# A decoder layer's expert stage: pairs of experts in rounds of 64 columns, changed to two expert streams in four equal groups of 32 columns, with a sorted load list and rolled loops

## The chip, the cores and the metric

One core of one Trainium2 chip runs the kernel. The metric is device time in microseconds for one launch. The core has TensorE (PE in the profile; PEld is its weight load), VectorE (DVE), ScalarE (ACT), GpSimd (POOL) and SyncE (SP), which here only issues DMAs.

## What is computed

One layer of a hybrid decoder for 512 prompt tokens and 8 sample tokens, d_model 1024, all in float32: adaLN modulation, an input projection to an RG-LRU half and a sliding-window attention half, an RMS norm of each half with a gain (`g_lru`, `g_attn`), an output projection, a residual layer norm, and then the expert layer, which the change is mostly about:

```python
def hier_moe(h, w_group, b_group, w_router, b_router, w_gate, w_up, w_down):
    pg = softmax(h @ w_group + b_group)                  # 4 groups
    g_val, g_idx = top_k(pg, 1)                          # one group for each token
    pe = softmax(logits of the 8 experts of that group)
    e_val, e_idx = top_k(pe, 2)                          # two experts in it
    weight = g_val * e_val / sum(e_val)
    expert = g_idx * 8 + e_idx                           # 32 experts
    z = silu(h @ w_gate[e]) * (h @ w_up[e]) * combine    # 1024 -> 256
    return sum over e of z @ w_down[e]                   # 256 -> 1024
```

520 tokens with two experts each are 1040 rows, over 32 experts of 3.15 MB of weights (three matrices of 1 MB), some 100 MB. The biases of the inputs make the groups unequal.

## The kernel before

The kernel is written engine by engine, with semaphores by hand; each engine's instructions run in the order of its function. The stages follow each other: modulation and input projection, LRU and attention, output projection with residual and norm in five tiles, router, expert stage, and the weighted sum of each token's two rows with the last norm.

**Attention half.** For each of four blocks of 128 queries VectorE masks scores (L1050), ScalarE makes exponentials (L770), TensorE transposes the weights, ScalarE evacuates these (L784), TensorE multiplies with the values (L1527) and VectorE's `store_O` copies the result out of PSUM into `yT` (L1076). After the last block ScalarE squares the four attention rows of `yT` (L795), TensorE sums the squares (L1577), VectorE makes a mean of the sums (L1114), multiplies the four attention rows with the gain `g_attn` (L1116) and takes a reciprocal (L1118), TensorE transposes it (L1583), and the output projection goes on (L1596).

**Routing.** VectorE finds the two experts of each token, TensorE counts the tokens of each expert and their ranks, and VectorE turns these into slots in a table in DRAM. The table has a column for each step and a row for each of the 128 columns of a step. Ten indirect stores by GpSimd write it (L590), one load brings it back (`idx_all`), and the gathers of token rows begin.

**Expert stage.** The 32 experts are 16 fixed pairs. A step handles up to 64 tokens of each expert of a pair: columns 0 to 63 belong to the one, 64 to 127 to the other. A pair with an expert of more than 64 tokens takes more steps. Three buffers hold a pair's weights each (`wex`, `SETS = 3`); SyncE loads pairs in order, gate and up when the gate-up of the pair that last used the buffer is done (`gu_ps`), down when its down projection is done (`y_ps`) (`load_pair`, L439 to L446). Two pairs and a part of the third are loaded ahead of the stage. On TensorE, step n does:

```python
for k in range(KD):                    # gate-up, L1680: 8 k-slices x 2 column groups
    for q in range(2):
        matmul(B[2 + j % 2][64*q : 64*q + 64, :], XT[:, j % 2, k, 64*q : 64*q + 64], gate and up of q, slice k)
transpose_X((j + 1) % RING, i, 0)      # first half of the next step's tokens, L1661
transposes of z                        # L1687, wait for silu (ACT, L842) and multiply (DVE, L1297)
transpose_X((j + 1) % RING, i, 1)
for k in range(2):                     # down, L1699: 2 k-slices x 2 banks x 2 column groups
    for c in range(2):
        for q in range(2): ...
```

The profile records each float32 matmul as two. VectorE and ScalarE copy half of y each (L1302, L849). GpSimd gathers the tokens of a step with an indirect DMA from `h_dram` into `X` (L608, L610) and scatters a step's y into `y_dram` with another (L619, L621). `X` and `yo` are rings of four (`RING`), the gather is three steps ahead (`AHEAD`): in each step GpSimd first gathers for step s + 3, then waits for the y copies of step s and scatters.

**Control.** Which buffer a step's pair lies in is known only on the chip: each step reads three registers (L1669 to L1671) and picks one of three arms by `If` (L1673). Four steps (a turn) are written out in the body of a loop; the first turn is peeled, three follow in a loop (L1708), and the rest up to `TURNS` = 8 stand in a loop whose body is guarded by `If(nturns > i)` (L1711, L1712). All engines go through the whole range and skip what isn't wanted (VectorE L1309, ScalarE L856, GpSimd L640). When GpSimd is through it waits for the last stores and sets `mark` (L648), SyncE reloads y (`yy`), and TensorE sums it (L1722).

## Time and profile before

| | us |
|---|---|
| median of three runs (662.65 to 664.29) | 663.6 |
| time of the profiled execution | 662.54 |
| its span, first to last instruction | 660.5 |
| PE busy | 539.1 (82%) |
| PEld busy | 274.0 (41%) |
| DVE busy | 229.9 (35%) |
| ACT busy | 159.1 (24%) |
| POOL busy | 124.3 (19%) |
| DMA, 168.97 MB | mean 256 GB/s |

The chain that ended last goes 63% by PE, 12% by DVE, 9% by DMA and 6% by the issue of DMAs on SyncE. Times in rows are microseconds from the first instruction; "mean ns" is that of one instruction. "128*64" is the shape of the part of TensorE's array that a matmul uses. An engine name with a q is its sequencer, which loads registers and branches ahead of the work that it has queued; such rows do not count as busy. In a row of a line's instructions three durations stand as least, median and most. "[4.13 <-DMA x]" is idle time of the engine ahead of the row and what ended it. For DMAs the last number is the time from issue to landing.

### The profile page before, as it was taken

What the parts mean: (1) busy time and instruction counts of PE and PEld (TensorE: products, weight loads), DVE (VectorE), ACT (ScalarE), POOL (GpSimd) and SP (SyncE); (2) the same over time, 40 slices, a digit from 0 to 9 for tenths busy, and PEclk for the clock granted to TensorE, in tenths of its full rate; (3) what the DMA queues carried; (4) which work ended last, traced back from release to release, by engine and by line L of the source; (5) the groups of instructions that cost most, each with busy time, mean ns of one, the idle gap of its engine ahead of it and who ended that gap; (6) DMA issues with size and microseconds to landing.
All of it is one profiled execution on the core that took longest, in us unless ns stands there. A gap on an engine that the chain in (4) does not pass through costs nothing.

```text
span 660.5 us, 7214 instructions
## 1 busy us (share of the span) xinstructions
PE 539.1 (82%) x2420; PEld 274.0 (41%) x2421; DVE 229.9 (35%) x524; ACT 159.1 (24%) x332; POOL 124.3 (19%) x186
## 2 busy tenths in 40 slices
PE   1879999999988799961079899989999978789391
PEld 0458777887434344430033334334333323233130
DVE  0331444323394588998011111111111101011178
ACT  1221444525465111220011111111211101011054
POOL 5020010000543440020621121112112111111000
PEclk9969999999799899986579999999999989789795
DMA  8993945401846812119379968249999999996432
GB/s 276 407 363 136 319 163 195 155 4 32 323 171 228 326 46 89 64 36 389 155 261 405 423 251 328 114 188 417 420 418 420 420 419 421 416 411 226 172 130 98
DMA packets 46004, 168.97 MB, mean 256 GB/s; under 512 B 13178, under 2 KB 22450, under 8 KB 30590
## 3 DMA queue, kind: packets, MB, share of 16 engines
q1 hardware_dynamic: 36682, 146.48, 56.6%
q0 software_dynamic: 8944, 21.87, 9.3%
q8 instruction: 27, 0.44, 0.3%
q10 hardware_dynamic: 340, 0.09, 0.1%
q14 instruction: 11, 0.09, 0.0%
HBM read 165.18 MB, written 18.32 MB: 278 GB/s over the span
## 4 chain that ended last, share of the span: by engine, by line
PE 63%; DVE 12%; DMA 9%; SPq 6%; issue 5%; ACT 3%; POOL 1%; POOLq 0%; DVEq 0%
PE B L1680 18%; PE B L1432 16%; PE B L1699 8%; PE B L1596 5%; DMA wex<-in_w_up 4%; PE B L1369 3%; SPq L372 3%; DMA x_tok<-in_x_sample 2%; PE B L1501 2%; SPq L374 1%; SPq L371 1%; PE B L1661 1%; PE B L1687 1%; PE B L1444 1%; PE B L1527 1%
## 5 line engine op out<-in xcount | busy, mean ns | idle before, releaser
L1680 PE MATMUL B<-wex,XT 128*64 128x512 f32 x640 | 149.7, 618 | 19.2 <-DMA wex<-in_w_up 11.2
L1432 PE MATMUL B<-hT,win 128*128 128x256 f32 (+1 forms) x448 | 104.1, 393 | 2.0 <-DVE hT L953 2.0
L1680 PEld LDWEIGHTS B<-wex,XT 128*64 128x64 f32 x640 | 52.9, 142 | 113.8 <-issue 112.0
L1432 PEld LDWEIGHTS B<-hT,win 128*128 128x128 f32 x448 | 86.2, 195 | 22.5 <-issue 9.3
L1699 PE MATMUL B<-wex,zT 128*64 128x512 f32 x320 | 73.1, 598 | 0.6
L1297 DVE TENSOR_TENSOR z<-silu_g,B 128x256 f32<-128x256 f32 x20 | 8.4, 422 | 162.0 <-ACT silu_g L842 162.0
L1661 PE MATMUL B<-ident,X 128*128 128x128 f32 x168 | 28.4, 294 | 26.8 <-DMA X<-h_dram,gidx 26.8
L1596 PE MATMUL B<-wout,yT 128*128 128x512 f32 x112 | 50.1, 605 | 0.0
L842 ACT ACTIVATE silu_g<-B 128x256 f32<-128x256 f32 x20 | 7.7, 386 | 153.5 <-PE B L1680 153.5
L1302 DVE COPY yo<-B 128x512 f32<-128x512 f32 x20 | 13.8, 692 | 83.1 <-PE B L1699 83.1
L619 POOL COPY sidx<-idx_all 128x1 int32 (+1 forms) x20 | 3.6, 182 | 198.8 <-DVE yo L1302 198.8
L1661 PEld LDWEIGHTS B<-ident,X 128*128 128x128 f32 x168 | 22.7, 196 | 43.1 <-issue 43.1
L1699 PEld LDWEIGHTS B<-wex,zT 128*64 128x64 f32 x320 | 21.2, 136 | 38.7 <-issue 34.3
L1596 PEld LDWEIGHTS B<-wout,yT 128*128 128x128 f32 x112 | 21.5, 195 | 26.6 <-issue 26.6
L1722 PE MATMUL B<-yy,wdiag 128*128 128x512 f32 (+1 forms) x40 | 21.5, 699 | 10.2 <-DMA yy<-y_dram 10.0
L610 POOL DMA_INDIRECT X<-h_dram,gidx x23 | 24.1, 1048 | 20.0 <-POOL gidx L608 18.8
L849 ACT ACTIVATE yo<-B 128x512 f32<-128x512 f32 x20 | 12.0, 598 | 62.2 <-PE B L1699 62.2
L565 POOL TENSOR_SCALAR P<-P,rden 128x256 f32<-128x256 f32 (+1 forms) x16 | 14.4, 914 | 59.4 <-DVE rden L1064 59.4
L1369 PE MATMUL B<-ada,cT 128*32 128x512 f32 x160 | 24.0, 704 | 1.7 <-issue 1.0
L621 POOL DMA_INDIRECT y_dram<-yo,sidx x20 | 20.3, 1016 | 17.3 <-POOL sidx L619 17.3
L1289 DVE COPY XT<-B 128x512 f32<-128x512 f32 x21 | 14.4, 684 | 20.3 <-PE B L1661 20.3
L534 POOL DMA_DIRECT2D ada<-in_w_ada x12 | 6.7, 563 | 77.5 <-PE B L1369 77.5
(327 smaller groups left out, 585.0 us busy)
## 6 DMA issues: line engine op xcount, KB each, us to landing
wex<-in_w_gate SPq DMA_DIRECT2D x32, 1024.0 KB, 16.8
wex<-in_w_up SPq DMA_DIRECT2D x32, 1024.0 KB, 19.3
wex<-in_w_down SPq DMA_DIRECT2D x32, 1024.0 KB, 20.4
ada<-in_w_ada POOLq DMA_DIRECT2D x12, 1024.0 KB, 7.4
ada<-in_w_ada SPq DMA_DIRECT2D x8, 1024.0 KB, 8.2
win<-in_w_in SPq DMA_DIRECT2D x7, 1024.0 KB, 14.0
wout<-in_w_out SPq DMA_DIRECT2D x1, 4096.0 KB, 13.1
yy<-y_dram SPq DMA_DIRECT2D x8, 512.0 KB, 6.7
```

The costliest lines, as they stand in the source:

```text
L372: sp.dma_start(to[:, q, KD * DE:GU], u_).then_inc(got, 16)
L565: pool.tensor_scalar(Pm[b % 3][:, h, keys], Pm[b % 3][:, h, keys], rden[:, b % 2, h:h + 1], None, ALU.mult).then_inc(P_ready, 1)
L610: pool.indirect_dma_start(X[:, j, :], None, h_dram[:, :], bass.IndirectOffsetOnAxis(ap=gidx[:, j:j + 1], axis=0), bounds_check=NT - 1, oob ...
L621: pool.indirect_dma_start(y_dram[:, :], bass.IndirectOffsetOnAxis(ap=sidx[:, j:j + 1], axis=0), yo[:, j, :], None, bounds_check=2 * NT - 1 ...
L1289: dve.tensor_copy(XT[:, s % 2, 0:4, :], B[0][:, :].rearrange("p (k m) -> p k m", m=P)).then_inc(XT_v, 1)
L1369: last = pe.matmul(B[7 if r == 2 else 4][32 * g:32 * g + 32, :], cT[:, k, :], w[:, g * 512:(g + 1) * 512], start=(k == 0), stop=(k == KD - 1))
L1432: last = pe.matmul(B[(q % 2) * 2 + h][:, 0:cn], win[:, n % 3, k, col:col + P], hT[:, k, c0:c0 + cn], start=(k == 0), stop=(k == KD - 1))
L1596: last = pe.matmul(B[2 * g + c][:, :], yT[:, FW * g + f, t * P:(t + 1) * P], wout[:, FW * g + f, c * 512:(c + 1) * 512], start=(f == 0), s ...
L1661: last = pe.transpose(B[half][:, (k % 4) * P:(k % 4 + 1) * P], X[:, j, k::KD], ident[:, :])
L1680: last = pe.matmul(B[2 + j % 2][64 * q:64 * q + 64, :], XT[:, j % 2, k, 64 * q:64 * q + 64], gu[:, :, k, :], start=(k == 0), stop=(k == KD ...
L1699: last = pe.matmul(B[5 + c][64 * q:64 * q + 64, :], zT[:, k, 64 * q:64 * q + 64], wex[pl][:, q, dn:dn + 512], start=(k == 0), stop=(k == 1))
L1722: last = pe.matmul(B[2 * (t % 2) + c][0:n, :], wdiag[0:n, t, e, 0:n], yy[0:n, t, e, c * 512:(c + 1) * 512], start=(e == 0), stop=(e == 1))
```

## The change

- The experts of group 0 (0 to 7) form stream A; the other 24 form 12 fixed pairs, stream B. A step works on one A expert in two lanes of 32 columns (rounds of `WA` = 64 tokens) and on one B pair in one lane each (rounds of `WB` = 32 tokens). Both streams advance by themselves; the number of steps is that of the longer. `MAXSTEP` becomes 44.
- Weights: three buffers for single A experts, the third in the place of the output projection's weights (region `w`), two for B pairs. Three A experts and two pairs are loaded ahead of or at the start of the stage. The 15 later loads are sorted on VectorE by the step that first needs them; SyncE reads the list entry by entry.
- `X`, `XT` and `yo` have one buffer each in place of four, two and four, in region `y`. GpSimd gathers for step s + 1 when step s's tokens are transposed, then scatters step s.
- All loops have one step as their body; TensorE has six arms (three A places times two B places) instead of three, and one loop from 0 to `MAXSTEP`.
- In the attention half `g_attn` is multiplied in as the results leave PSUM (`gA`), and ScalarE squares each block out of PSUM once VectorE has stored it; the four multiplications behind the sums go.

```diff
-CAP = 64
...
-RING = 4
-AHEAD = RING - 1
...
+NA, NB = EPG, (NE - EPG) // 2
+NU = NA + NB
+WA, WB = 64, 32
+
+MAXSTEP = max((2 * NT + (WA - 1) * NA) // WA, (2 * NT + (WB - 1) * NB) // WB)
+MINSTEP = max(NA, NB)
...
+ABUF, BBUF = 3, 2
...
-        X = row("X", [P, RING, D], "w", 0)
-        XT = row("XT", [P, 2, KD, P], "w", 16384)
+        X = row("X", [P, D], "y", 0)
+        XT = row("XT", [P, KD, P], "y", 8192)
...
-        yo = row("yo", [P, RING, D], "y", 0)
+        yo = row("yo", [P, D], "y", 4096)
...
+        wA = [row("wA0", [P, EXW], "r", 0), row("wA1", [P, EXW], "r", 4 * EXW), row("wA2", [P, EXW], "w", 0)]
+        wB = [row("wB0", [P, 2, EXW], "x", 0), row("wB1", [P, 2, EXW], "r", 8 * EXW)]
...
-            sp.wait_ge(lgT_ps, 2)
-            load_expert(2, 1, 0)
+            sp.wait_ge(L_ps, TT + 1)
+            sp.wait_ge(A_ps, TT)
+            load_a(2)
+            sp.wait_ge(x1_stored, 16 * (TT + 1))
+            load_b(0, 0)
+            load_b(0, 1)
             sp.wait_ge(lg_ps, 1)
...
-            load_expert(3, 1, 1)
...
-            load_expert(4, 2, 0, (True, False))
-            sp.wait_ge(X_in[AHEAD - 1], 16)
-            load_expert(4, 2, 0, (False, True))
-            load_expert(5, 2, 1)
+            load_b(1, 0)
+            sp.wait_ge(X_in, 16)
+            load_b(1, 1)
...
+            with sp.Fori(0, LATER) as n:
+                free = sp.value_load(loads_i[0:1, 1, bass.ds(n, 1)], min_val=1, max_val=MAXSTEP)
+                place = sp.value_load(loads_i[0:1, 2, bass.ds(n, 1)], min_val=0, max_val=ABUF + BBUF - 1)
+                e = sp.value_load(loads_i[0:1, 3, bass.ds(n, 1)], min_val=0, max_val=NE - 2)
...
+                for b in range(BBUF):
+                    with sp.If(place == ABUF + b):
+                        sp.wait_ge(gu_ps, free)
+                        for q in range(2):
+                            later_expert(e + q, wB[b][:, q, :], (True, False), wB_in[b])
+                        sp.wait_ge(y_ps, free)
+                        for q in range(2):
+                            later_expert(e + q, wB[b][:, q, :], (False, True), dB_in[b])
...
+            def one(s):
+                pool.wait_ge(XT_ps, counted(2 * s + 2))
+                gather(s + 1, 2 * s + 1)
+                scatter(s)
+
+            gather(0, 0)
+            one(0)
+            with pool.Fori(1, MINSTEP) as s:
+                one(s)
...
+            nsteps = pool.value_load(steps_i[0:1, 0:1], min_val=MINSTEP, max_val=MAXSTEP)
+            with pool.Fori(MINSTEP, MAXSTEP) as s:
+                with pool.If(nsteps > s):
+                    one(s)
+
+            ends = [pool.value_load(ends_i[0:1, j:j + 1], min_val=16 * MINSTEP, max_val=16 * (MAXSTEP + 1)) for j in range(2)]
+            pool.wait_ge(y_out, ends[0])
+            pool.wait_ge(X_in, ends[1])
...
+            def squares(b):
+
+                act.wait_ge(O_stored, 2 * (b + 1))
+                act.activation(qT[:, :, b * P:(b + 1) * P], B[6][:, :].rearrange("p (g q) -> p g q", q=P), ACT.Square).then_inc(sq_ready, 1)
+
             for b in range(TT + 1):
                 if b < TT:
                     exps(b)
+                if b >= 2:
+                    squares(b - 2)
                 if b >= 1:
                     evacuate_PT(b - 1)
...
-            for f in range(FW, 2 * FW):
-                act.activation(sq[:, f, :], yT[:, f, :], ACT.Square).then_inc(sq_ready, 1)
+            squares(TT - 1)
...
-                        i = dve.tensor_copy(yT[64 * half:64 * half + 64, FW + 2 * kv:FW + 2 * kv + 2, b * P:(b + 1) * P],
...
+                        i = dve.tensor_tensor(yT[64 * half:64 * half + 64, FW + 2 * kv:FW + 2 * kv + 2, b * P:(b + 1) * P],
...
-            for f in range(FW, 2 * FW):
-                dve.tensor_scalar(yT[:, f, :], yT[:, f, :], par[:, 32 + f:33 + f], None, ALU.mult).then_inc(yg_ready, 1)
...
+                    pe.wait_ge(sq_ready, FW + b)
...
+            def lanes(a, b):
+
+                return [wA[a], wA[a], wB[b][:, 0, :], wB[b][:, 1, :]]
+
+            def one(n):
+                arm = pe.value_load(arm_i[0:1, bass.ds(n, 1)], min_val=0, max_val=ABUF * BBUF - 1)
...
+                for a in range(ABUF):
+                    for b in range(BBUF):
+                        with pe.If(arm == BBUF * a + b):
...
+                            pe.wait_ge(wA_in[a], need_a)
+                            pe.wait_ge(wB_in[b], need_b)
                             for k in range(KD):
...
+                                for g, w in enumerate(lanes(a, b)):
+                                    gu = w[:, 0:GU].rearrange("p (c k f) -> p c k f", c=2, k=KD)
+                                    last = pe.matmul(B[2][32 * g:32 * g + 32, :], XT[:, k, 32 * g:32 * g + 32],
                                                      gu[:, :, k, :], start=(k == 0), stop=(k == KD - 1))
                             last.then_inc(gu_ps, 1)
...
+                            pe.wait_ge(X_in, 16 * n + 32)
+                            transpose_X(0)
                             pe.wait_ge(z_ready, n + 1)
...
+            nsteps = pe.value_load(steps_i[0:1, 0:1], min_val=MINSTEP, max_val=MAXSTEP)
+            with pe.Fori(0, MAXSTEP) as n:
+                with pe.If(nsteps > n):
+                    one(n)
```

## Rows read from the trace of the kernel before

**Rows 1.** Page, part 2: 40 equal slices of the span.
```profile
DMA  8993945401846812119379968249999999996432
GB/s 276 407 363 136 319 163 195 155 4 32 323 171 228 326 46 89 64 36 389 155 261 405 423 251 328 114 188 417 420 418 420 420 419 421 416 411 226 172 130 98
```

**Rows 2.** Timeline, first gate-up of the expert stage.
```profile
336.50 8.49 PE L1680 MATMUL B<-wex,XT 128*64 128x512 f32 x32 [0.73 <-ACT XT L836]
```

**Rows 3.** Timeline, behind the last step.
```profile
616.37 1.04 POOL L621 DMA_INDIRECT y_dram<-yo,sidx  x1 [0.86 <-POOL sidx L619]
...
619.17 0.10 POOL L648 MEMSET mark<- 128x1 f32 x1 [1.76 <-DMA y_dram<-yo,sidx]
...
624.37 2.04 PE L1722 MATMUL B<-yy,wdiag 128*128 128x512 f32 x2 [10.01 <-DMA yy<-y_dram]
```

**Rows 4.** Timeline of one step, all engines: start, duration, engine, line.
```profile
423.50 0.71 PE L1661 MATMUL B<-ident,X 128*128 128x128 f32 x4
...
424.51 0.51 PE L1687 MATMUL B<-ident,z 128*128 128x128 f32 x2 [0.29 <-DVE z L1297]
...
425.49 3.65 PE L1699 MATMUL B<-wex,zT 128*64 128x512 f32 x16
...
429.19 0.69 DVE L1302 COPY yo<-B 128x512 f32<-128x512 f32 x1 [4.13 <-PE B L1699]
...
431.15 1.02 POOL L621 DMA_INDIRECT y_dram<-yo,sidx  x1 [0.86 <-POOL sidx L619]
...
433.21 1.05 POOL L610 DMA_INDIRECT X<-h_dram,gidx  x1 [0.84 <-POOL gidx L608]
```

**Rows 5.** DMA issues, one gather each, windows 415:428, 402:415 and 441:454.
```profile
X<-h_dram,gidx POOLq DMA_INDIRECT x1, 3.3
...
X<-h_dram,gidx POOLq DMA_INDIRECT x1, 8.3
...
X<-h_dram,gidx POOLq DMA_INDIRECT x1, 9.7
```

**Rows 6.** Chain that ended last: modulation in four lanes, clock low, then full.
```profile
174.06 6.03 PE B L1369 x32
...
186.42 1.85 PE B L1369 x16
```

**Rows 7.** Timeline of PE, two gate-ups behind waits for weights.
```profile
536.61 8.78 PE L1680 MATMUL B<-wex,XT 128*64 128x512 f32 x32 [4.13 <-DMA wex<-in_w_up]
...
552.94 7.09 PE L1680 MATMUL B<-wex,XT 128*64 128x512 f32 x32 [1.98 <-DMA wex<-in_w_up]
```

**Rows 8.** Page, part 3, then sequencer rows of single lines: arms, loops.
```profile
q8 instruction: 27, 0.44, 0.3%
...
L1673 PEldq COMPARE_BRANCH  x60: 68/207/5084, 336.0 to 611.2; - x60
...
L1708 PEldq COMPARE_BRANCH  x3: 76/207/223, 440.8 to 547.5; - x3
...
L1711 PEldq ALU_OP  x4: 36/36/36, 611.4 to 613.8; - x4
...
L640 POOLq ALU_OP  x4: 32/32/32, 616.1 to 617.5; - x4
```

**Rows 9.** Timeline, attention's third block and what follows the last.
```profile
204.05 1.78 DVE L1076 COPY yT<-B 64x256 f32<-64x256 f32 x4 [1.33 <-PE B L1527]
...
204.63 1.09 ACT L784 ACTIVATE PT<-B 128x512 f32<-128x512 f32 x2 [2.70 <-PE B L1518]
...
215.76 5.93 DVE L1116 TENSOR_SCALAR yT<-yT,par 128x520 f32<-128x520 f32 x4
...
223.46 0.69 PE L1583 MATMUL B<-ident,rs 128*128 128x128 f32 x2 [4.47 <-DVE rs L1118]
```

**Rows 10.** DMA issues, stores of the table, windows 313.5:315 and 324:325.
```profile
table<-pair_id,slot POOLq DMA_INDIRECT x2, 6.2
...
table<-pair_id,slot POOLq DMA_INDIRECT x1, 1.9
```

More of the change, by code:

```diff
@@ L195, in build @@
         par = small("par", [P, 40])
+        gA = small("gA", [P, G])
         stT = small("stT", [P, FW, 32])
@@ L405, in _ @@
             sp.wait_ge(win_ps, 2 * len(ORDER))
-            for q in range(2):
-                load_expert(q, 0, q)
+            for i in range(2):
+                load_a(i)
             sp.wait_ge(ss_sum_ps, 1)
@@ L625, in turn @@
-            def turn(i, peeled):
-                for j in range(RING):
-                    s = RING * i + j
-                    if not (peeled and j == 0):
-                        pool.wait_ge(XT_ps, counted(2 * s))
-                    gather((j + AHEAD) % RING, s + AHEAD, AHEAD + 2 * s)
-                    scatter(j, s)
-            for s in range(AHEAD):
-                gather(s, s, s)
-            turn(0, True)
-            with pool.Fori(1, MINTURNS) as i:
-                turn(i, False)
@@ L638, in _ @@
-            pool.wait_ge(steps_ready, 1)
-            nturns = pool.value_load(turns[0:1, 0:1], min_val=MINTURNS, max_val=TURNS)
-            with pool.Fori(MINTURNS, TURNS) as i:
-                with pool.If(nturns > i):
-                    turn(i, False)
-            scattered, gathered = counted(16 * nturns, 16 * nturns + 16)
-            for j in range(RING):
-                pool.wait_ge(y_out[j], scattered)
-                pool.wait_ge(X_in[j], gathered if j < AHEAD else scattered)
-            pool.memset(mark[:, :], 0.0).then_inc(experts_done, 1)
+                pool.tensor_copy(sidx[:, :], idx_all[:, bass.ds(s, 1), 1]).then_inc(idx_ready, 1)
@@ L860, in row_stats @@
+            copy_XT(0)
+            one(0, True)
+            with act.Fori(1, MINSTEP) as n:
+                one(n, False)
+            nsteps = act.value_load(steps_i[0:1, 0:1], min_val=MINSTEP, max_val=MAXSTEP)
+            with act.Fori(MINSTEP, MAXSTEP) as n:
+                with act.If(nsteps > n):
+                    one(n, False)
             def row_stats(t, n):
@@ L1093, in _ @@
                 if b == 1:
+                    for kv in range(NKV):
+                        for half in range(2):
+                            step(dve.tensor_copy(gA[HD * kv:HD * kv + HD, half::2],
+                                                 par[HD * half:HD * half + HD, 32 + FW + 2 * kv:32 + FW + 2 * kv + 2]))
+                    settle()
                     dve.wait_ge(sO_ps, 1)
@@ L1243, in _ @@
[L1243 to L1247 removed]
+            step(dve.tensor_scalar(unum_i[:, 0, 0:NA], B[5][:, 0:NA], 1.0, float(WA - 1), ALU.max, ALU.add))
+            link(dve.tensor_reduce(umax[:, NA:NU], B[5][:, NA:NE].rearrange("p (a b) -> p a b", b=2), AX.X, ALU.max))
@@ L1279, in _ @@
[L1279 to L1284 removed]
+            step(dve.tensor_copy(uend_i[:, :], uend[:, :]))
@@ L1313, in _ @@
+            copy_XT(0)
+            one(0, True)
+            with dve.Fori(1, MINSTEP) as n:
+                one(n, False)
+            nsteps = dve.value_load(steps_i[0:1, 0:1], min_val=MINSTEP, max_val=MAXSTEP)
+            with dve.Fori(MINSTEP, MAXSTEP) as n:
+                with dve.If(nsteps > n):
+                    one(n, False)
             for t, n in TILES:
```

388 lines of the change are left out of this document (204 added, 184 removed).

## The prediction

> **What bounds the kernel now.** I read the forty slices of the page first, to find the stretch that matters: from about 330 us on the kernel is in its expert stage, and there the DMA engines are full from slice 28 to 36 at 411 to 421 GB/s but not in slices 24 to 27, where they carry 328, 114 and 188 GB/s [rows 1]. So neither engine binds throughout: while experts 4 to 7 take three steps a pair, TensorE binds and the weight stream sleeps; after that the stream binds. The stage runs from the first gate-up at 336.5 us [rows 2] to 614.4 us (the last output store is issued at 616.4, 2.0 us behind the last matmul) [rows 3], 277.9 us for 20 steps, and 46.1 us follow it. Then one step in order of time, for the chain that the change shortens to one buffer: transposes of the next tokens, of z, the down projection of 3.65 us, the y copy, the store of y issued 2.0 us after the last matmul, and the gather of tokens issued 4.1 us after it [rows 4]. Now this gather is three steps early, so nobody sees how long it takes. Last, how long it takes: 3.3 us from issue to landing where the weight queue is empty, 8.3 us with it just filled, 9.7 us with it full [rows 5].
>
> **Fewer steps.** The reference's router on its inputs gives experts 0 to 7 these tokens: 57 29 51 33 137 103 163 91; the pairs behind them have maxima 25 11 20 14 20 40 39 36 7 9 7 6. Before: sixteen pairs in rounds of 64, 20 steps (two with three rounds). After: stream A needs 1+1+1+1+3+2+3+2 = 14 rounds of 64, stream B 1+1+1+1+1+2+2+2+1+1+1+1 = 15 rounds of 32; they run beside each other, so 15 steps.
>
> **A step on TensorE.** Four lanes of 32 columns replace two of 64. The page has four such lanes elsewhere: two chunks of the modulation, 16 records, take 1.85 us [rows 6], 0.925 us for one k-slice of four lanes. Gate-up: 8 x 0.925 = 7.4 us (7.1 now [rows 7]); down: 4 x 0.925 = 3.7 us. Between gate-up and down lie 1.99 us [rows 4]. Sequencer work between steps (three register loads, up to five skipped arms, the loop's branch) hides under the down projection as now; I add 1.1 us exposed for the longer chain of arms. A step on TensorE alone: 1.1 + 7.4 + 2.0 + 3.7 = 14.2 us.
>
> **The gather, now late.** There is one X and one yo. GpSimd issues the gather of step n+2 only after the store of step n. Issue is 4.1 us after the last matmul of step n, 4.3 with its loop's branch. Landing is between 3.3 and 9.7 us, as weights are in flight or not; I take 9.0 under load. TensorE wants it 1.1 + 7.4 = 8.5 us after that last matmul, and it comes at 13.3: a hole of 4.8 us in the middle of the step. Behind it are the transposes (0.72 us without their wait on z, then 0.98) and down 3.7: 5.4 us. A hole of such length also lowers the granted clock: the gate-up behind 4.13 us idle took 8.78 us against 7.09 behind 1.98 us [rows 7], so 1.7 us. A loaded step: 4.3 + 9.0 + 5.4 + 1.7 = 20.4 us. Who else waits on that one X: only TensorE; the single yo asks for a store that lands about 10 us after the step before, which is early.
>
> **Which steps are loaded.** After the seven experts that are in place, 25 of 3.15 MB remain, at 420 GB/s 7.5 us each, 187 us, and some 20 us for X and y. The first steps free A and a pair together (22.5 us of transfers in a step of 20.4), so steps 1 to 5 are loaded. Later a step frees a pair or nothing. Behind a short step that freed one, the gather meets gate, up and down in full: steps 9 and 11. Behind a long step only the down part is left: steps 6, 7, 12 and 13, between 14.2 and 20.4, I take 16.0. Behind the second round of a pair nothing moves: steps 8, 10, 14, 14.2 us. Step 0 starts at the low clock as now, 8.49 us of gate-up [rows 2]: 14.6. Sum: 14.6 + 7 x 20.4 + 4 x 16.0 + 3 x 14.2 = 264.0 us, against 277.9: 13.9 us less, although five steps of about 13.9 went. The weights are no bound: 207 us of transfers in 264.
>
> **The end of the loops.** Nobody says stop: each engine walks the range to MAXSTEP, now 44, and skips. Before, three turns were skipped; now 29 steps. A skip costs GpSimd (617.5 - 616.1) / 3 = 0.47 us and TensorE (613.8 - 611.4) / 3 = 0.8 us [rows 8]. GpSimd's begin 1.7 us after the last matmul: 1.7 + 29 x 0.47 + 1.6 for two register loads = 16.9 us until the mark that releases the reload of y, which stood at 4.8 us (619.17) [rows 3]. TensorE's last 23.2 us but begin 3 us before that matmul, so they end at 20.2, ahead of the y that lands at 22.1 instead of 10.0 [rows 3]. Cost: 12.1 us, cover none. The Trainium skill (Advanced Engine Details and Errata, Control Flow Timing) gives about 108 ns to a compare-and-branch; two of them 29 times would be 6.3 us on each engine and the cost would be 3 to 5 us, an estimate from that page. The spacing in the rows counts the whole iteration, and the sum goes by it.
>
> **Ahead of the stage.** The gain of the attention half moves into the copies out of PSUM, so the four VectorE scalings of 5.93 us go; TensorE idled 4.47 us for what stood behind them, and all of that is won [rows 9]. Against it: ScalarE's square of a block now waits for VectorE's store (204.05 + 1.78) and stands ahead of the next evacuation, which began at 204.63 [rows 9]: 1.8 us in the third block, 0.2 in the second, and 0.4 for the extra copies of the samples. Net 2.0 us won (bounds 0 and 4.5). Routing: five more small VectorE operations ahead of the slots, 0.8 us; the some 35 more behind them (sorting loads) take 8 us and end some 10 us before X lands. More weights are asked for in this window: 12.6 MB from 295 us, until 325. GpSimd's last table store, at 324.0 now, then meets them; loaded ones took 6.2 us, it takes 1.9 now [rows 10]: I take 2.3 more, bounds 0 and 4.3. SyncE is moved past nothing that it waits for. Together 1.1 us lost.
>
> **Sum.** -13.9 + 1.1 + 12.1 = -0.7 us. The profiled execution has 660.5 us span and 662.54 us of time, so 661.8; the median of the runs is 1.1 higher, 663.6, and I forecast 663. 0.3% (2 us) is about what a measurement of this kernel can tell from no change.
>
> **Rivals.**
> (a) The late gather as above (0.54), 663; by itself 645 to 682: landing at 8.3 takes 7 us off, at 9.7 it adds 6, an exposed 3 us between steps adds 4, no clock loss takes 9 off. This case lies on both sides.
> (b) The gather is not late (0.15): with weights in flight only 80% of the time it lands in about 3.3 us, steps go at 14.2 and the last weights set the end. Some 223 us of stage (207 of transfers and the ends): 41 less, 622. Against it: 8.3 us already stood where the queue had been filled only 5 us before.
> (c) Slower: the clock (0.25). The hole is in the middle of a step, and behind it come sparse transposes, so the low level lasts through the down projection. At the low level four lanes need 1.5 us (6.03 / 4) for what takes 0.925 [rows 6], so down costs 6.0 and the transposes 0.9 more: 3.2 in place of 1.7 us, in nine steps with a hole: 13.5 us, 676. It decides from 2.0 us per hole on. For it: step 0, where transposes after a long idle did not lift the clock and the gate-up still lost 1.4 us (8.49 against 7.09) [rows 2, 7].
> (d) Slower: code loading (0.06). TensorE took up to 5.08 us in one branch over an arm, but 0.08 to 0.22 in the loop's own branch back [rows 8]; the queue of instructions moved 27 packets, 0.44 MB in all, once per piece of code [rows 8]. If each step lost 2.4 us twice, all 15 steps would take about 20.3 us: 304 us, 703. The Trainium skill (Runtime: NRT & Kernel Launch, Instruction fetch mechanics) says that a taken branch out of the fetched window stalls for a fetch, and would make this the likely case with a jump in every step; the trace's loop of twelve arms, larger than the new one of six, ran back without it.
> Chances: (a) gives 0.26 faster, 0.13 same, 0.15 slower; with (b), (c) and (d): faster 0.41, same 0.13, slower 0.46. Range 642 to 685: it holds (a) and (c), and leaves out (b) and (d).
>
> **What would show it.** 15 silu and 15 yo copies. TensorE's transposes of X wait on the DMA of X, 4 to 5 us in steps 1 to 5 and next to nothing in 8, 10 and 14; if these waits are absent, (b). Gate-up near 7.4 us, down near 3.7; down near 5 or 6 means (c). Stage near 264 us. Mark some 17 us after the last matmul, y's sum some 22 us after it; if it stays at 10, the skip price is wrong. Scalings of yT gone and 4.47 us of idle with them. Gaps over 2 us between down and gate-up with the weights landed would mean (d). Wrong altogether would be a step count other than 15, or weights as the last wait through the middle of the stage.

## The result and the profile after

The changed kernel takes 702.1 us (median of 4 runs, 696.4 to 703.3) beside 663.9 us of the kernel before: ratio 1.0565, 95% interval 1.0490 to 1.0639, so some 5.7% slower. The 663.9 is the median of four runs, of which one took 1134.0 us; the ratio leaves that one out, and the other three have 663.6. The forecast was 663 with a range of 642 to 685, and 0.46 for slower.

The profiled execution's span is 701.2 us, 40.7 more than before. Three stretches hold them. The stage begins at 337.85 us instead of 336.50 [rows 2]: 1.35 us more. It lasts until the last matmul at 643.2: 305.4 us instead of 277.9, 27.5 more. And 58.0 us follow instead of 46.1: 11.9 more. The first and the last are what the prediction said (1.1 and 12.1). The stage should have come to 264.0 and took 41.4 us more than that.

The page of the kernel after, slices of 17.5 us (the stage is slices 19 to 36, counted from 0), the instruction queue, and the two parts that name the stage's costs, the chain and the groups:

```profile
PE   1889999998979998600814865658696867774091
...
PEclk9979999999899999855765988999889898988585
...
GB/s 278 403 370 101 324 127 234 65 0 244 251 97 419 44 91 62 112 423 268 285 414 136 315 423 416 413 421 202 353 66 412 182 405 362 360 101 84 112 161 92
...
q8 instruction: 15, 0.25, 0.1%
...
PE 50%; DMA 19%; issue 12%; DVE 11%; ACT 3%; POOL 2%; POOLq 2%; SPq 0%; DVEq 0%
...
L1761 PE MATMUL B<-wA,XT 128*32 128x512 f32 x480 | 112.8, 624 | 49.5 <-issue 49.5
...
L1740 PE MATMUL B<-ident,X 128*128 128x128 f32 x128 | 29.4, 373 | 79.2 <-DMA X<-h_dram,gidx 79.2
...
L1780 PE MATMUL B<-wA,zT 128*32 128x512 f32 x240 | 64.0, 682 | 0.2
```

Before, the DMA engines stood at 411 to 421 GB/s in nine slices on end [rows 1]; now they do so in four. PE is at 9 in one slice of the stage alone, and its granted clock is below 9 tenths in eleven of the eighteen. So through most of the stage neither the matmuls nor the weights set the pace. L1740, the transposes of X, wait 79.2 us for the gather (30.1 of them once, ahead of the stage). And L1761, the gate-up, waits 49.5 us for "issue", time in which the engine waited for nothing that the profile shows. More than half of that is one piece. Timeline of all engines from the end of step 0, the SyncE queue left out (start, duration, engine, line; in brackets the idle time before it and what ended it):

```profile
353.07 0.69 DVE L1378 COPY yo<-B 128x512 f32<-128x512 f32 x1 [4.14 <-PE B L1780]
...
356.99 1.05 POOL L645 DMA_INDIRECT X<-h_dram,gidx  x1 [0.84 <-POOL gidx L643]
378.41 1.07 PE L1761 MATMUL B<-wA,XT 128*32 128x512 f32 x2 [25.41 <-issue]
```

Between step 0 and step 1 TensorE stands still for 25.41 us. Its sequencer rows on L1753, the `If` over the arms, in three windows (count; ns least/median/most; first and last start):

```profile
L1753 PEldq COMPARE_BRANCH  x2: 5690/5986/6281, 350.7 to 357.0; - x2
...
L1753 PEldq COMPARE_BRANCH  x2: 5638/5648/5658, 362.8 to 368.5; - x2
...
L1753 PEldq COMPARE_BRANCH  x78: 68/200/217, 394.5 to 640.7; - x78
```

Four branches, at 350.7, 357.0, 362.8 and 368.5 us, take 6.28, 5.69, 5.64 and 5.66 us: 23.3 us, of which the first 2.3 lie under the down projection. The 4.2 us from the last of them to the first matmul are the sequencer's ordinary work for a step: the branch back, three table loads of 0.30 us with their register operations (374.8 to 377.2), and the short branches to the arm. In the later steps most of this lies under the down projection: 21.9 us of it show in 13 steps, 1.7 each (1.1 predicted). Later, 78 branches of the same line take 217 ns at most. From 353 to 378 us the instruction queue moves 5 packets, 0.08 MB; I read them as the code of arms that step 0 did not run. The same stretch as a window (length; busy time of PE, PEld, DVE, ACT, POOL; then granted clock, DMA share and GB/s):

```profile
353.00:378.40 25.40, 0.00 (x0) 0.02 (x1) 0.69 (x1) 0.60 (x1) 2.44 (x4) 0.57 0.83 340
```

TensorE does nothing in it, its clock is granted at 0.57, near the lower of its two levels (1.2 of 2.4 GHz), and the weights go on at 340 GB/s in the mean (400 from 357 to 374 us, next to nothing after that).

The other steps, from the y copies of VectorE (L1378): steps 2 to 14 last 22.8, 21.3, 20.7, 20.6, 14.6, 22.0, 13.9, 20.9, 14.5, 22.5, 15.1, 21.8 and 18.7 us. Step 2, the chain of waits in order of time:

```profile
396.93 0.21 POOL gidx L643
397.25 0.49 issue
397.78 0.19 issue
397.96 10.89 DMA X<-h_dram,gidx
408.90 1.12 PE B L1740 x4
410.02 0.43 PE B L1768 x2
410.44 0.85 PE B L1740 x4
411.30 5.28 PE B L1780 x32
416.60 0.04 DVEq L1377
```

The gather is issued 4.2 us after step 1's last matmul, lands 10.89 us later, and all behind it follows at once. The ten later landings on this chain take 10.2, 9.9, 9.9, 10.3, 4.3, 9.9, 11.1, 5.6, 9.7 and 8.2 us. Last, what follows the stage, GpSimd's mark and TensorE's sum, where [rows 3] had them at 619.17 and 624.37:

```profile
645.30 1.01 POOL L655 DMA_INDIRECT y_dram<-yo,sidx  x1 [0.86 <-POOL sidx L653]
659.33 0.19 POOL L676 TENSOR_TENSOR mark<-mark 128x1 f32<-128x1 f32 x1 [13.01 <-issue]
664.69 3.75 PE L1800 MATMUL B<-yy,wdiag 128*128 128x512 f32 x4 [21.52 <-DMA yy<-y_dram]
```

### The profile page after: what moved, and what is told of

It is laid out like the page before. It is cut to its first block, busy times and chain, and to the rows that moved or that the text cites. A ratio compares the mean times of both kernels' runs of the same rounds, so it can differ in the third digit from the quotient of the medians.

```text
span 701.2 us, 8747 instructions
## 1 busy us (share of the span) xinstructions
PE 492.4 (70%) x2850; PEld 251.3 (36%) x2851; DVE 223.7 (32%) x544; ACT 149.0 (21%) x313; POOL 107.7 (15%) x167
## 4 chain that ended last, share of the span: by engine, by line
PE 50%; DMA 19%; issue 12%; DVE 11%; ACT 3%; POOL 2%; POOLq 2%; SPq 0%; DVEq 0%
DMA X<-h_dram,gidx 15%; PE B L1508 15%; PE B L1780 9%; PE B L1670 5%; PE B L1761 5%; PE B L1740 3%; PE B L1445 3%; DMA x_tok<-in_x_sample 2%; PE B L1577 2%; DVE yo L1378 1%; PE B L1639 1%; PE B L1520 1%; PE B L1800 1%; PE B L1768 1%; POOL table L625 1%
## 5 line engine op out<-in xcount | busy, mean ns | idle before, releaser
L1761 PE MATMUL B<-wA,XT 128*32 128x512 f32 x480 | 112.8, 624 | 49.5 <-issue 49.5
L1761 PE MATMUL B<-wB,XT 128*32 128x512 f32 x480 | 112.8, 625 | 0.0
L1508 PEld LDWEIGHTS B<-hT,win 128*128 128x128 f32 x448 | 86.3, 195 | 22.5 <-issue 9.3
L1740 PE MATMUL B<-ident,X 128*128 128x128 f32 x128 | 29.4, 373 | 79.2 <-DMA X<-h_dram,gidx 79.2
L1761 PEld LDWEIGHTS B<-wA,XT 128*32 128x32 f32 x480 | 33.8, 114 | 125.3 <-issue 125.3
L1780 PE MATMUL B<-wA,zT 128*32 128x512 f32 x240 | 64.0, 682 | 0.2
L1780 PE MATMUL B<-wB,zT 128*32 128x512 f32 x240 | 64.0, 682 | 0.0
L1740 PEld LDWEIGHTS B<-ident,X 128*128 128x128 f32 x128 | 22.1, 210 | 92.6 <-DMA X<-h_dram,gidx 60.8
L1800 PE MATMUL B<-yy,wdiag 128*128 128x512 f32 (+1 forms) x40 | 21.5, 699 | 21.7 <-DMA yy<-y_dram 21.5
L1378 DVE COPY yo<-B 128x512 f32<-128x512 f32 x15 | 10.4, 692 | 72.9 <-PE B L1780 72.9
L1367 DVE COPY XT<-B 128x512 f32<-128x512 f32 x16 | 11.0, 690 | 69.5 <-PE B L1740 69.4
L1780 PEld LDWEIGHTS B<-wA,zT 128*32 128x32 f32 x240 | 14.1, 124 | 39.6 <-issue 35.3
L1761 PEld LDWEIGHTS B<-wB,XT 128*32 128x32 f32 x480 | 27.7, 114 | 0.0
L599 POOL TENSOR_SCALAR P<-P,rden 128x256 f32<-128x256 f32 (+1 forms) x16 | 14.5, 918 | 59.9 <-DVE rden L1094 59.9
L879 ACT ACTIVATE yo<-B 128x512 f32<-128x512 f32 x15 | 9.0, 597 | 56.4 <-PE B L1780 56.4
## 6 DMA issues: line engine op xcount, KB each, us to landing
wA<-in_w_gate SPq DMA_DIRECT2D x8, 1024.0 KB, 12.7
```

The costliest lines, as they stand in the source:

```text
L599: pool.tensor_scalar(Pm[b % 3][:, h, keys], Pm[b % 3][:, h, keys], rden[:, b % 2, h:h + 1], None, ALU.mult).then_inc(P_ready, 1)
L879: act.activation(yo[:, 512:D], B[6][:, :], ACT.Copy).then_inc(y_a, 1)
L1367: dve.tensor_copy(XT[:, 0:4, :], B[0][:, :].rearrange("p (k m) -> p k m", m=P)).then_inc(XT_v, 1)
L1378: dve.tensor_copy(yo[:, 0:512], B[5][:, :]).then_inc(y_v, 1)
L1508: last = pe.matmul(B[(q % 2) * 2 + h][:, 0:cn], win[:, n % 3, k, col:col + P], hT[:, k, c0:c0 + cn], start=(k == 0), stop=(k == KD - 1))
L1740: last = pe.transpose(B[half][:, (k % 4) * P:(k % 4 + 1) * P], X[:, k::KD], ident[:, :])
```

## The experiments

Three theories, one for each loss. **Skips**: the tail's 12 us are 29 passes that are tested and skipped. **Code**: the hole of 25.4 us is the fetching of arms, once, and each fetch is slow since weights fill the DMA engines. **Order**: the long steps are the gather's, and not for being slow but for being issued behind the end of the step before. Times are medians; after each, the ratio to the kernel before, with its interval.

### e1_range15: nothing to skip

```diff
-            with pool.Fori(MINSTEP, MAXSTEP) as s:
+            with pool.Fori(MINSTEP, 15) as s:
```
and so for ScalarE, VectorE and TensorE.

> The change, with the loops over steps of all four engines ending at 15 instead of 44: these inputs make 15 steps, so nothing of the work is left out, only the 29 passes that each engine skips. Main theory (skipped passes cost 0.47 us each on GpSimd, 0.8 us on TensorE, and lie on the path behind the last step): GpSimd's mark comes 3 us behind the last matmul instead of 16.1, the last down projection stays near 643 us, the tail of 58.0 us shrinks by 12 to 46, and the time by 12 us, 702 to 690. Rival (the skips run beside the last scatter's landing and the last weights' wait, so something else is late next): under 4 us gained.

689.4 us (1.0405, 1.0381 to 1.0430), 12.7 less. The profiled execution is the shortest of the five, 684.85 us. GpSimd's last scatter and mark, and TensorE's sum:

```profile
638.93 1.06 POOL L656 DMA_INDIRECT y_dram<-yo,sidx  x1 [0.86 <-POOL sidx L654]
641.81 0.19 POOL L677 TENSOR_TENSOR mark<-mark 128x1 f32<-128x1 f32 x1 [1.82 <-DMA y_dram<-yo,sidx]
647.22 12.95 PE L1801 MATMUL B<-yy,wdiag 128*128 128x512 f32 x25 [10.44 <-DMA yy<-y_dram]
```

13.01 us of "issue" before the mark have become 1.82 us behind the scatter, and TensorE's wait for y 10.44 instead of 21.52. The mark is 5.0 us behind the last matmul (3 were expected; before it was 4.8), and 46 us follow that matmul instead of 58.0. The skips were the tail's whole loss; the late gathers (45.4 us of waits in 11 steps) and the hole (26.4 us here) stayed.

### e2_dry15: the code fetched ahead of the stage

```diff
+            pool.memset(arm_i[:, 0:1], ABUF * BBUF).then_inc(warm, 1)
...
-            with pe.Fori(0, 15) as n:
-                one(n)
+            pe.wait_ge(warm, 2)
+            with pe.Fori(0, 15 + 1) as m:
+                one(m)
...
+                with pe.If(arm == ABUF * BBUF):
+                    pe.wait_ge(steps_ready, 1)
+                    pe.wait_ge(X_in, 16)
+                    transpose_X(0)
+                    transpose_X(1)
```
The tables `arm_i` and `wneed` are moved by one place, and the waits in the arms go by m instead of n + 1.

> As the kernel whose loops end at 15, with one pass more at the start of TensorE's loop, taken as soon as the rank matmuls are out (about 307 us), in which none of the six arms is true; a seventh arm then waits for the first rows and transposes them. The work is the same. Main theory (the 25.4 us hole behind step 0 is code of the six arms being fetched at 5.7 us each while the weights fill the DMA engines, once): the hole goes, the fetches fall into TensorE's idle time before the first gather lands at 333.6 and hold the first gate-up up by 0 to 9 us: 16 to 25 us less than the kernel without this pass, 665 to 674. Rival 1 (the hole is a wait for the second step's weights, loads that the trace names badly): the hole stays at 353, no gain. Rival 2 (code is fetched again at every turn of the loop): later steps keep whatever they pay, and the hole comes back in step 1 in part.

666.5 us (1.0040, 1.0016 to 1.0064), 22.9 less than without the extra pass. Branches of the extra pass, and the gate-ups of steps 0 and 1:

```profile
L1757 PEldq COMPARE_BRANCH  x2: 5820/6015/6210, 306.1 to 312.0; - x2
...
L1757 PEldq COMPARE_BRANCH  x2: 4938/5368/5798, 318.3 to 324.1; - x2
...
L1757 PEldq COMPARE_BRANCH  x1: 3358/3358/3358, 329.1 to 329.1; - x1
```
```profile
337.37 1.07 PE L1765 MATMUL B<-wA,XT 128*32 128x512 f32 x2 [1.21 <-ACT XT L872]
...
355.39 0.62 PE L1765 MATMUL B<-wA,XT 128*32 128x512 f32 x2 [2.61 <-issue]
```

The five slow branches now start at 306 to 329 us, where TensorE waits for the first gather anyway, and the last ends at 332.5, before its transposes begin at 334.21. The first gate-up follows these 3.2 us later (337.37; 3.8 without the extra pass), and the second begins 2.61 us behind step 0. Both rivals fall: the hole is no wait for weights, and the code does not leave again (from 334 us on no branch of the line takes more than 214 ns). That the gain is under the 26.4 us of the hole is the gather: it landed inside the hole in step 1, and now step 1 waits for it like the others (20.9 us, 41.1 without the extra pass).

The five also show what traffic does to a fetch: 5.82, 6.21 and 5.80 us while the DMA engines move 424, 417 and 412 GB/s, 4.94 us at 191, and 3.36 us at 47.

### e5_quiet: the same fetches with the DMA engines nearly empty

```diff
+            sp.wait_ge(gu_ps, 2)
             with sp.Fori(0, LATER) as n:
```
on top of e1_range15.

> As the kernel whose loops end at 15, but SyncE sends the first later weights only when the gate-up of step 1 is done, instead of that of step 0. Nothing is left out. Main theory (the hole behind step 0 is four or five fetches of TensorE's code, 5.7 us each because the weight transfers fill the DMA engines): with the queues empty each fetch takes 2 to 3 us and the hole of 26.4 us comes to 9 to 13; the second step ends 14 to 17 us earlier; the weights then start late by one step, so at the end 0 to 14 us are left of it (675 to 690). Rival (the length of a fetch is its own, whatever the queues do): the hole stays at 25, and the time goes to about 690 or above, for the later weights.

698.1 us (1.0514, 1.0476 to 1.0552), above the expected 675 to 690. TensorE's branches, a window over the hole, and the gate-up of step 1:

```profile
L1755 PEldq COMPARE_BRANCH  x2: 3041/3076/3110, 350.9 to 354.0; - x2
...
L1755 PEldq COMPARE_BRANCH  x2: 2978/3198/3418, 357.2 to 360.7; - x2
```
```profile
353.00:368.00 15.00, 0.26 (x4) 0.00 (x0) 0.69 (x1) 0.60 (x1) 2.46 (x4) 0.63 0.16 51
```
```profile
368.05 1.07 PE L1763 MATMUL B<-wA,XT 128*32 128x512 f32 x2 [14.79 <-issue]
```

The four fetches take 3.04, 3.11, 3.42 and 2.98 us, 12.5 together instead of 23.3, with 51 GB/s in flight instead of 340. So the weights nearly double a fetch. What they do not explain is 3 us each, and the 4.4 us between the last slow branch and the first matmul, which are the sequencer's table loads and short branches as in the change (4.2 there). The hole is 14.8 us, above the 9 to 13 expected: step 1 ended 8.5 us earlier than in e1_range15, not 14 to 17. And the time got worse, since the postponed weights were then missing: TensorE waits 32.7 us for them in four later steps, where e1_range15 has no such wait. Keeping the queues quiet is no cure.

### e3_order: the gather ahead of the scatter

```diff
-                pool.wait_ge(XT_ps, counted(2 * s + 2))
-                gather(s + 1, 2 * s + 1)
+                pool.wait_ge(XT_ps, counted(2 * s + 4))
+                gather(s + 2, 2 * s + 2)
                 scatter(s)
...
             gather(0, 0)
+            pool.wait_ge(XT_ps, 2)
+            gather(1, 1)
             one(0)
```
The counts behind it move by one, and `NSTEP` grows by one. X stays a single buffer: it is free in the middle of a step, as soon as it is transposed. The change makes GpSimd stand in the scatter's wait for y at that moment.

> The change, with GpSimd's order turned round: rows for step s+2 are gathered as soon as those of s+1 are transposed, ahead of the scatter of step s, where the change gathers s+1 only after the scatter of s-1 has waited for the end of that step. Loops still end at 44. Main theory (ten to twelve steps are long because the gather goes out 4.2 us behind a step's end and lands 10 us later): the gather goes out about 3 us before a step's end, 7 us earlier, and steps of 21.5 us come to about 14.5; then the weights bind (25 experts of 3.1 MB in about 225 us from 347.6, so until 573) and the last down projection ends near 600: about 43 us less, 658, with 630 as the end where the weights don't bind. Rival (the gather is only slow, not late: it lands 7 us later for being issued in the densest weight traffic): landings of 15 us or more, under 20 us gained, 682 or more.

650.8 us (0.9809, 0.9785 to 0.9833), 51.3 less where 43 were expected: 1.9% under the kernel before, from an order of two calls. One step, all engines but the gate-up's and the queue's rows:

```profile
499.95 0.72 PE L1742 MATMUL B<-ident,X 128*128 128x128 f32 x4
...
503.17 1.05 POOL L645 DMA_INDIRECT X<-h_dram,gidx  x1 [0.83 <-POOL gidx L643]
...
505.75 0.69 DVE L1380 COPY yo<-B 128x512 f32<-128x512 f32 x1 [4.24 <-PE B L1782]
...
507.71 1.02 POOL L655 DMA_INDIRECT y_dram<-yo,sidx  x1 [0.86 <-POOL sidx L653]
```

The gather goes out 2.6 us before the y copy instead of 4.0 behind it. No transpose of X in the stage waits for it any more; in the change those waits were 49.1 us in 11 steps (79.2 less the 30.1 ahead of the stage). One wait for weights, 5.5 us, has come in their place, in a step of 20.5 us; the others behind step 1 last 13.8 to 16.5. The rival falls: the gathers land 8.4 us after their issue in the median of 13, not 15 or more, and nobody waits for them.

### e6_order15 and e4_all: the parts together

e6_order15 is e3_order and e1_range15, e4_all has the extra pass of e2_dry15 as well.

> The gather ahead of the scatter, and loops that end at 15, without the extra pass. Main theory (the tail's 12.7 us are behind everything and add in full): 650.8 - 12.7 = 638.1, with the hole of 26 us still behind step 0 and few waits for weights after it, which were loaded meanwhile; so the extra pass is worth 13 us here and not 23, since the DMA engines bind the kernel that has all three. Rival (the skipped passes of the four engines hid something in this order too): 643 or more.

641.4 us (0.9661, 0.9627 to 0.9694), 9.4 less than e3_order: between the two expectations, and nearer to the rival's bound of 643. In the profiled executions TensorE's sum of y begins 11.8 us earlier (602.40 instead of 614.21) and the span is 10.5 us shorter; where the other 1.3 us go is open.

> All three together: loops that end at 15, the extra pass before the stage, and the gather ahead of the scatter. Main theory: the tail's 12 us go in full; the hole's 24 us and the late gathers' 60 us are both in the stage, where the weight transfers (until about 573 at the earliest) bind next, so they don't add: the last down projection at 590 to 600, the time 636 to 648, faster than the kernel before. If the three simply added, 702 - 12 - 20 - 43 = 627. Rival (the weights bind from the first step on, so that the hole was hidden behind them): no better than the reordered kernel less 12, 646.

624.8 us (0.9437, 0.9409 to 0.9466), 5.6% under the kernel before. The page's DMA slices, and TensorE's waits in the stage (in total, times, longest):

```profile
GB/s 281 404 348 213 253 231 197 157 57 0 216 297 46 306 288 68 68 70 95 419 373 253 338 426 419 423 422 419 423 421 334 354 352 411 416 409 226 202 107 103
```
```profile
PE B L1746 <- DMA X<-h_dram,gidx: 30.1, 1, 30.1
PE B L1767 <- issue: 23.4, 12, 2.7
PE B L1767 <- DMA wB<-in_w_up: 15.3, 2, 13.0
```

From 23 on, seven slices stand at 419 to 426 GB/s. That is below the expected 636 to 648, and even below the 627 of the plain sum, since the order alone gave 51.3 us where the sum had 43. With the measured parts (12.7, 22.9 and 51.3) the plain sum is 615.2, so the parts do overlap, but by 9.6 us: 3.3 of the skips and 6.3 of the extra pass, which is worth 16.6 us here and not 22.9. A step of 27.5 us waits 13.0 for weights, since TensorE now starts on them while the stream has only begun.

### e8_dyn and e9_general: loop ends from a register

Fifteen written into a loop is right for these inputs only. e8_dyn is the change with

```diff
-            with pool.Fori(1, MINSTEP) as s:
-                one(s)
...
-            with pool.Fori(MINSTEP, MAXSTEP) as s:
-                with pool.If(nsteps > s):
-                    one(s)
+            with pool.Fori(1, nsteps) as s:
+                one(s)
```
and so for the other engines (TensorE's from 0). e9_general adds the order of e3_order and the extra pass, in which TensorE loads the end of its own loop.

> The change with loops whose end is the number of steps read from a register, instead of passes up to 44 that are tested and skipped. It computes all that the change does, for any routing. Main theory (the skipped passes alone make the tail long): the same 12.7 us as with loops that end at 15 by hand, 689.4. Rival (a loop end in a register costs each turn something, or the first turn of the loop waits for the value): 692 or more.

686.2 us (1.0352, 1.0290 to 1.0414), the same as e1_range15 within the intervals: the whole cost of the skips goes without 15 in the code.

> The version for any routing: the gather ahead of the scatter, loop ends read from a register on all four engines (TensorE reads its own in the extra pass), and the extra pass ahead of the stage. Main theory: nothing in it costs more than in the kernel with 15 written in, so 624.8, within 2 us, 5.9% under the kernel before. Rival (TensorE's register load behind the wait for the number of steps delays the first transposes): 627 to 630.

633.2 us (0.9536, 0.9493 to 0.9578), 8.4 above e4_all: a miss. TensorE's idle time between two steps grew by 0.3 to 0.4 us (2.10 to 2.47, 1.84 to 2.22), some 5 us in 15 steps, and from 445 to 585 us the same 954 matmul records keep it busy for 117.4 us instead of 114.1. The sequencer's rows show the first part. In e9_general each of the three register loads of a step has two rows of a bounds check (SEQ_ASSERT), in e4_all and e8_dyn one, and the loads with their checks take 2.4 us (442.2 to 444.6) instead of 2.1 (441.6 to 443.7):

```profile
L1754 PEldq SEQ_ASSERT  x9: 18/18/18, 442.2 to 559.7; - x9
```
```profile
L1744 PEldq SEQ_ASSERT  x18: 18/18/18, 442.2 to 566.9; - x18
```

A likely reason, not tried, is that the end of TensorE's loop is here a plain register, whose range the code does not state, while e8_dyn's is a value read with its bounds. The second part is the clock: of eight steps from 428 us on, four have a granted clock of about 0.9 (0.89 to 0.90) in e9_general and two (0.88 and 0.90) in e4_all, where the others have 1.00, and such a step keeps TensorE busy for 14.0 us instead of 12.3. Whether the longer idle time brings the lower clock stays open.

### The third buffer: e10_two_a_plain, e7_two_a, e11_two_a_order

Two buffers for single experts, so four arms; `ABUF, BBUF = 2, 2`, no `load_a(2)` ahead of the stage, and the round is unit / 2. e10 does this to the change itself, e7 to e4_all.

> The change itself (702.1 us) with two buffers for single experts instead of three, nothing else altered; TensorE's loop has four arms instead of six. Main theory (late gathers set the steps, so the third buffer is worth nothing here, and two arms fewer are 10 us of code less to fetch, one or two fetches of 5.7 us): 691 to 697, faster than with three. Rival (the single experts' weights come late with two buffers): the waits for weights grow by 7 us or more, and the time is 702 or above.

681.7 us (1.0256, 1.0201 to 1.0311): without its third buffer the change is 20.4 us faster, where 5 to 11 were expected. The gate-up of step 1, and the branches that are slow:

```profile
359.78 1.07 PE L1760 MATMUL B<-wA,XT 128*32 128x512 f32 x2 [11.99 <-issue]
```
```profile
L1752 PEldq COMPARE_BRANCH  x2: 4390/4936/5481, 345.5 to 351.0; - x2
```

Two slow branches instead of four, and 12.0 us of hole instead of 25.4: 13.4. Step 0 ends 5.2 us earlier, at 347.86: one expert fewer is in front of the routing's own transfers. The last table store is issued 2.6 us earlier, and the wait for it is 1.86 us instead of 4.61. The 13 steps behind take 248.1 us instead of 249.4. No weights are missed (1.1 us in all).

> The kernel with all three edits (624.8 us), with two buffers for single experts instead of three: the third, in the place of the projection's weights, isn't used, and the order of loads is worked out for two. Main theory (the stage is bound by the DMA engines, and the third buffer's worth is one expert's 3.1 MB loaded before the stage, 7.5 us at 420 GB/s): 7 to 10 us slower, 632 to 635. Rival 1 (a buffer less makes loads wait for buffers as well, so that the DMA engines idle between): 15 to 30 us slower, 640 to 655. Rival 2 (single experts are never late, the paired stream alone binds): within 2 us of 624.8.

629.0 us (0.9456, 0.9418 to 0.9494) beside 624.8: 4.2 more by the medians, 1.3 by the ratios, with intervals that overlap, and below the 632 to 635 of the main theory. Even where gather and code no longer hide it, the third buffer's worth is not the 7.5 us that I gave it, and may be nothing.

> A simpler version for any routing, without the extra pass: two buffers for single experts, so four arms, the gather ahead of the scatter, loop ends read from a register. Main theory (the hole is as long as the arms that are fetched in it, 12 us with four; part of it is taken back later, because the weights bind and go on loading meanwhile, as the six-arm version without the extra pass lost 16.6 us for a hole of 26): 4 to 8 us above the two-buffer version with the extra pass (629.0), 633 to 637. Rival (with two buffers the loads can't run ahead in the hole, since both buffers are held, so that all of it stays): 640 or more.

630.2 us (0.9498, 0.9459 to 0.9537): two buffers, the turned order, loop ends from a register, no extra pass; right for any routing, and simpler than the change. That is below the expected 633 to 637. With a hole of 12.5 us it is as fast as e7_two_a within the intervals, so less of the hole is left over than I gave it.

### before_attn: the attention part alone

The change's edits to the attention half, made to the kernel before.

> The kernel before with the change's attention part alone: the scaling by g_attn in the copies out of PSUM, the squares taken from PSUM by ScalarE, the four scalings behind the attention gone, and the transposes of the sums placed ahead of the output projection. Main theory (the predicted term): the output projection starts 2.0 us earlier and what follows moves with it, 663.6 to 661.6, and the 1.9 us by which the changed kernel's projection came earlier is this part alone. Rival (the stage behind it waits for weights that are loaded at their own pace, so the head start is lost there): within 0.5 us of the kernel before.

661.6 us (0.9957, 0.9933 to 0.9982) in 12 runs: 2.3 less than before by the medians, 2.9 by the ratio. The output projection begins at 221.8 instead of 224.2 us:

```profile
L1608 PE MATMUL B<-wout,yT x112: 592/592/697, 221.8 to 275.9; 128*128 128x512 f32 x112
```

## Why the prediction was wrong

**The sum that it made.** The forecast was 663 because 13.9 us won in the stage should have paid for 12.1 at its end. Of the 41.4 us that the stage took beyond 264.0, step 0 has 0.6, step 1 20.4, the six other steps called loaded 6.3, the four called middle 9.5, and the three called short 4.6. So half of it is a hole that the sum had at nothing, and half are terms of the gather that were too small. By the sum, either half alone would have left the time just inside the range, at some 684.

**The step that failed: code loading stood in the sum at nothing (rival (d), 0.06).** It was put aside by this sentence: "the trace's loop of twelve arms, larger than the new one of six, ran back without it". That is true of turns once made, and e2_dry15 shows it for the new loop too: code stays. But it says nothing of the first passage. Before, arms that were passed for the first time also had slow branches: 2.93 us at 375.9, 2.36 at 425.9, 5.08 at 562.4 and 2.67 at 584.2. The prediction read the 5.08 of [rows 8] as a maximum, without the moment at which it fell, which is the first step of the last loop:

```profile
L1673 PEldq COMPARE_BRANCH  x1: 5084/5084/5084, 562.4 to 562.4; - x1
```

There they came one at a time and partly under a down projection, and TensorE stood idle for at most 2.3 us behind them, or 4.8 beside a wait for weights. In the change four come in a row, behind step 0, while SyncE puts nine transfers of 1 MB into the queues (347.6 to 358.2). Rival (d) priced them as 2.4 us twice in each of 15 steps (703 in all); its 20.3 us a step do not follow from the terms shown, which give 14.2 + 4.8 = 19.0. That the measured total is near 703 is luck: it is 23.3 us, four times 5.8, in one step, and the rest is the gather's. The Trainium skill (Runtime: NRT & Kernel Launch, Instruction fetch mechanics) says that a taken branch out of the fetched window stalls for a fetch. The trace agrees for the first turn (5.64 to 6.28 us each); later turns of the same branches take at most 0.22 us, so a jump in every step is no stall in every step.

**The gather, case (a): the second half.** The mechanism was right in all its steps: issue 4.1 to 4.2 us after the last matmul (4.3 predicted), the wait in the middle of the step, and some 7 us from landing to the end of the step (5.4 + 1.7 predicted; 7.7 in step 2). Its size was off in two terms. Landing under load takes 10.2 us in the mean of the eight rows of over 9 us, not 9.0; the upper bound, 9.7, was exceeded in seven of eleven. And more steps are loaded: 7 and 13 at 22.0 and 21.8 us (I took 16.0), 14 at 18.7 (I took 14.2). From step 6 on short and long ones alternate; of the four that I called middle two were short (14.6, 15.1) and two long. The steps that are not late last 13.9 to 15.1, about as predicted (14.2).

**The clock, case (c).** The hole in the middle does cost clock, and in the down projection, not in the gate-up where my 1.7 us had it: the gate-up stays at 7.1, the down took 5.28 in step 2 and its matmuls 682 ns in the mean against 595 in e4_all. But the lower level (1.07 us a record, 0.60 at the higher) ended within the down, halfway in step 2 and after a quarter in step 3, so the 6.0 us of rival (c) did not come either. In all, a late gather cost 1.0 us in the down (mean of nine steps, against 3.69) and 0.7 in the transposes (2.40 against 1.66). That is the 1.7 us of the sum: right in size, wrong in place. The clock is not what made the forecast wrong.

**What held.** Fifteen steps. Four lanes: down 3.64 us where the clock is full (3.7 predicted), gate-up 7.11 (7.4). The price of a skip, and the tail it makes: mark at 16.1 us behind the last matmul (16.9), sum at 21.5 (22.1), 11.9 us lost (12.1); e1_range15 gives 12.7 back. The 3 to 5 us that followed from the Trainium skill (Advanced Engine Details and Errata, Control Flow Timing) were too few: a whole pass costs more than its two branches, 0.44 us each by e1_range15 (12.7 us for 29). The attention part: 2.0 us predicted, 2.3 measured alone. The last table store under weight traffic takes longer: 5.2 us from issue to landing (4.2 predicted), of which GpSimd waits 4.61. The stage began 1.35 us later, for 1.1.

**What was asked wrongly.** I summed the change as it stood and never asked which of its losses were of its idea. None was of the lanes (the six arms come from the two streams, but not the moment at which they are fetched): equal lanes in 15 steps, with the gather ahead of the scatter, give 641 and 625 us, below the 663.9 of the kernel before. (How much the kernel before would gain by a loop end in a register was not tried; it skips three turns and has 46.1 us behind its stage, e4_all 45.5.) The 5.7% are an order of two calls (51.3 us alone), code fetched at the worst moment (22.9), and passes skipped (12.7), less what these hide of one another.

## What to carry to other kernels

With one buffer left, put the refill at the moment the buffer is free, not where the other work of its engine ends: a wait that stands first in an engine's program delays all behind it, and here that cost more than the change could win. Look at the first turn of a loop with arms by itself: code comes in once, each piece at the price of a transfer in the traffic of that moment, so let it come while the engine waits for something else, and count arms as a cost of buffers. And end a loop at a count in a register rather than skip to a maximum; look at the step afterwards, since e8_dyn paid nothing for it and e9_general stayed 8.4 us above the kernel with 15 written in.

## What the runs showed that was not expected

A branch of TensorE that fetches code takes 3.0 to 3.4 us with some 50 GB/s in flight (e5_quiet, and the last in e2_dry15), 4.9 with 191, and 5.5 to 6.5 with 390 and more (the change, e1_range15, e3_order, e2_dry15); a packet of the instruction queue has 16 KB or so (0.08 MB in 5). It does not hold everywhere: in the kernel before, two slow branches took 2.9 and 2.7 us with over 400 GB/s in flight, and why is open.

A buffer more made the kernel slower by 20.4 us, through two arms of code and one early load.

The weight queue pushes back on the engine that issues. In e4_all, SyncE's rows for one pair:

```profile
377.11 0.35 SPq L461 DMA_DIRECT2D wB<-in_w_gate  x1
377.55 0.38 SPq L462 DMA_DIRECT2D wB<-in_w_up  x1
378.13 1.20 SPq L461 DMA_DIRECT2D wB<-in_w_gate  x1
379.42 2.08 SPq L462 DMA_DIRECT2D wB<-in_w_up  x1
382.53 8.12 SPq L464 DMA_DIRECT2D wB<-in_w_down  x2
```

The same issue takes 0.35 us with little outstanding and 2 to 4 us each when several experts are. The DMA engines are full there (419 to 426 GB/s), so I take it that this cost nothing, but whatever SyncE had to do behind it would have waited.
